# A residual block ended row tile by row tile: how the output projection hands over to the feed-forward

## The chip, the cores and the metric

The kernel runs on one core of a Trainium2 chip. The metric is the device time of one execution in microseconds (us). The kernel before was run three times: 2187.65 us median, 2186.25 lowest, 2188.59 highest. One more execution was profiled; it took 2188.95 us, of which the profile's span covers 2187.3.

## The reference, cut to what matters

The reference chains two transformer blocks over 256 tokens of width 2048, all in fp32. The change sits in the second block, between its output projection and its feed-forward:

```python
x  = x + gt1 * (y @ w_out)                       # residual, 256 x 2048
h2 = rmsnorm_2(x, g_norm2) * (1 + sc2) + sh2     # needs all 2048 columns of a row
u  = h2 @ w_up                                   # 2048 x 11008
x  = x + gt2 * ((silu(conv3x3(u_gate) + conv_b) * u_val) @ w_down)
return rmsnorm_2(x, g_final)
```

`rmsnorm_2` divides each row by the root of the mean of its squares, so a row's norm waits for the last column block of the projection, but no row waits for another row.

## The kernel before, in words

**Tiles.** The 256 tokens are two row tiles `rt` of 128. A product of 256 x 2048 with a column block of 512 is cut into 8 units. A unit is 256 rows of the weight, two slices `kk` of 128. Every fp32 operand is split in two fp32r parts, high and low, and a product takes three matmuls of 128 x 512 (high-high, high-low, low-high). So a unit is 2 slices x 2 row tiles x 3 = 12 matmuls, a block is 96, and they add up in one PSUM buffer `gemm_ps[:, bank, rt]`; blocks alternate between two buffers.

**Weights.** SyncE fetches each unit into one of 4 slots (`w_raw`). ScalarE writes the high part (`w_hi`, L624), VectorE the low part (`w_lo`, L1053). ScalarE may write a slot only when TensorE has finished the unit that had it before: unit n waits for `used` of unit n-4.

**Activations.** Rows are scaled by their inverse root (ScalarE, L641, `rows_set`), transposed by TensorE in groups of two 128-column chunks (L1890, `ps[:, g % 2]`, `tr_ps`), scaled and shifted by VectorE into `tmpT` (L1085, `tr_val`), copied to the high part `a_hi` by ScalarE (L635, `tr_hi`) and taken off to the low part `a_lo` by VectorE (L1093, `tr_lo`). Unit i of the feed-forward's first block needs group i.

**Order.** Each engine runs one list of instructions written out by hand; semaphores tie the lists together, and an engine waits at the first instruction whose semaphore isn't there. The output projection (`U_OUT2`) has 4 column blocks. After the fourth, VectorE multiplies each row tile by the gate and adds it to the residual (`last_block`, L1109 and L1110), ScalarE takes the squares of the last block (`last_square`, L775), VectorE sums the parts and finds the inverse root of both tiles (`sum_of_parts` and `roots`, L1104 and L1063 to L1070), ScalarE scales the rows, and TensorE transposes groups 0 and 1. Then the first feed-forward block begins, with group i+2 transposed after unit i. 21 more blocks and the down projection follow, back to back. The last block of the down projection is already taken tile by tile (`by_tile`, `tile_ps`): the last four units run for tile 0 and then for tile 1, and `tile_root` (L1114 on) finds each tile's root by itself.

Of the kernel before, what the change touches and what calls it, by code (L numbers as in the profile page):

```python
# [5 lines left out]
F32 = mybir.dt.float32  # L6
# [7 lines left out]
P = 128  # L14
# [199 lines left out]

class Count:
# [16 lines left out]
def build(nc, a):  # L232
# [102 lines left out]
    cw = at("cw", [P, 10 * FCH], F32, 200.75)  # L335
    cwr = at("cwr", [P, 4, P], F32, 202.5)
# [53 lines left out]
    with nc.Block() as block:  # L390
# [218 lines left out]
        def _(act):  # L609
# [352 lines left out]
            for c in range(DC):  # L962
                for i in range(2, 10):
                    if c == 0 and i - 2 >= Y_AHEAD:
                        turned("y", i - 2)
                    splits(U_OUT2 // SLOTS + 2 * c, i, i + 1)
# [5 lines left out]
            for rt in range(RT):  # L972
                last_square(rt, xres, lambda rt: y[:, rt, (DC - 1) * NBLK:DC * NBLK], 1)
# [22 lines left out]
            def ffn_block(b, par, start=2, finish=2):  # L996
                for i in range(2, 10):
                    if isinstance(b, int) and b == 0:
                        if i == 2:
                            act.wait_ge(S("root_set"), 3)  # L1000
                            scaled_rows(y, xres, 0)
                            scaled_rows(y, xres, 1)
                        if i in (4, 6):
                            scaled_rows(y, xres, i // 2)
                        turned("x2", i - 2)
# [7 lines left out]
            ffn_block(0, 0, 0, 0)  # L1013
# [24 lines left out]
            for rt in range(RT):  # L1038
                last_square(rt, x2_sb, lambda rt: squares[:, rt], 2)
                act.wait_ge(S("root_out"), rt + 1)  # L1040
# [5 lines left out]
        def _(dve):  # L1046
# [611 lines left out]
            for c in range(DC):  # L1658
                for i in range(2, 10):
# [5 lines left out]
                    splits(U_OUT2 // SLOTS + 2 * c, i, i + 1)  # L1665
# [751 lines left out]
```

## Time and profile before

| | us |
|---|---|
| median of three runs | 2187.65 |
| profiled execution | 2188.95 |
| its span | 2187.3 |
| TensorE busy (matmul) | 2138.5 |
| VectorE busy | 1493.5 |
| ScalarE busy | 1054.3 |
| last matmul of the output projection starts | 1434.45 |
| first feed-forward matmul starts | 1446.40 |
| first matmul of the second feed-forward block starts | 1473.72 |

Busy times are sums over the span. The last three rows are times from the span's start; between them lies the stretch that the change touches. The profile gives TensorE's granted clock as a fraction of its upper level of 2.4 GHz, so 0.50 is the lower level of 1.2 GHz.

### The profile page before, as it was taken

The page shows a single profiled execution, that of the slowest core. Times are in us where ns is not written, and L with a number is a line of the kernel's source. Part 1 is how long each engine was busy: PE and PEld are TensorE (multiplying, and loading weights), DVE is VectorE, ACT ScalarE, POOL GpSimd, SP SyncE. Part 2 cuts the span into 40 slices and gives each one's busy share as a digit, 9 for nine tenths or more (in the row PEclk, how much of TensorE's full clock was granted, in tenths as well). Part 3 has the DMA queues.
Part 4 walks back from the last instruction along what each step waited for, and adds up shares of the span by engine and source line. Part 5 has one row for each costly group of instructions (what it writes and reads, how often), then busy time and mean ns, then how long its engine had stood idle before and what let it go on. Part 6 is the DMA issues. An engine that isn't in the chain of part 4 may idle for free.

```text
span 2187.3 us, 28818 instructions
## 1 busy us (share of the span) xinstructions
PE 2138.5 (98%) x10067; PEld 1734.2 (79%) x10067; DVE 1493.5 (68%) x2213; ACT 1054.3 (48%) x1317; POOL 50.3 (2%) x97
## 2 busy tenths in 40 slices
PE   7999999999999999999999999989999999999998
PEld 6777778888787777877788887868888888888886
DVE  6456657967676787776665777567787777775454
ACT  5343435654444444445633655445555555554443
POOL 0000000000001100000000000000000000000000
PEclk9999999999999999999999999989999999999999
DMA  8877768967777969976443436555556565567664
GB/s 313 280 274 252 261 237 286 345 237 261 240 275 250 334 222 353 320 257 203 144 125 103 134 108 221 185 194 185 181 183 191 177 198 177 183 194 244 192 194 141
DMA packets 279801, 484.18 MB, mean 221 GB/s; under 512 B 21630, under 2 KB 112864, under 8 KB 277648
## 3 DMA queue, kind: packets, MB, share of 16 engines
q1 hardware_dynamic: 274544, 464.93, 63.7%
q0 software_dynamic: 5152, 17.84, 2.3%
q8 instruction: 67, 1.10, 0.2%
q14 instruction: 38, 0.31, 0.0%
HBM read 476.23 MB, written 6.48 MB: 221 GB/s over the span
## 4 chain that ended last, share of the span: by engine, by line
PE 86%; DVE 6%; issue 3%; DMA 3%; ACT 2%; SPq 0%; ACTq 0%; DVEq 0%
PE gemm_ps L1805 75%; DVE w_lo L1053 2%; DMA w_raw<-in_w_in_dram 2%; ACT w_hi L624 2%; PE ps L1849 1%; DMA w_raw<-in_w_out_dram 1%; PE ps L2213 1%; DVE tmpT L1085 1%; PE ps L2351 1%; DVE msum L1220 1%; PE ps L2282 1%; PE ps L1890 0%; PE ps L2236 0%; PE ps L2235 0%; PE ps L1858 0%
## 5 line engine op out<-in xcount | busy, mean ns | idle before, releaser
L1053 DVE TENSOR_TENSOR w_lo<-w_raw,w_hi 128x1024 fp32r<-128x1024 f32 (+1 forms) x688 | 827.4, 1215 | 467.8 <-ACT w_hi L624 461.2
L1805 PE MATMUL gemm_ps<-w_hi,a_hi 128*128 128x512 f32 (+1 forms) x2304 | 916.4, 398 | 18.2 <-DVE w_lo L1053 9.3
L624 ACT ACTIVATE w_hi<-w_raw 128x1024 fp32r<-128x1024 f32 (+1 forms) x688 | 710.1, 1050 | 464.5 <-PE gemm_ps L1805 325.5
L1805 PE MATMUL gemm_ps<-w_hi,a_lo 128*128 128x512 f32 (+1 forms) x2304 | 897.1, 389 | 0.0
L1805 PE MATMUL gemm_ps<-w_lo,a_hi 128*128 128x512 f32 (+1 forms) x2304 | 896.1, 389 | 0.0
L1805 PEld LDWEIGHTS gemm_ps<-w_hi,a_hi 128*128 128x128 f32 x2304 | 434.3, 188 | 133.8 <-issue 25.5
L1805 PEld LDWEIGHTS gemm_ps<-w_hi,a_lo 128*128 128x128 f32 x2304 | 433.8, 188 | 91.9
L1805 PEld LDWEIGHTS gemm_ps<-w_lo,a_hi 128*128 128x128 f32 x2304 | 434.7, 189 | 84.2 <-issue 0.5
L1708 DVE SCALAR_TENSOR_TENSOR acc<-gp,cw,acc 128x256 f32<-128x256 f32 x344 | 151.5, 481 | 13.8 <-DVE acc L1708 1.4
L1220 DVE SCALAR_TENSOR_TENSOR msum<-mraw,cs,msum 128x1024 f32<-128x1024 f32 x120 | 153.3, 1277 | 1.2 <-DMA mraw<-in_w_mod_dram 0.4
L1805 PE MATMUL gemm_ps<-w_hi,ft_hi 128*128 128x512 f32 x344 | 134.2, 390 | 2.2 <-DVE w_lo L1053 2.2
L1805 PE MATMUL gemm_ps<-w_lo,ft_hi 128*128 128x512 f32 x344 | 133.9, 389 | 0.0
L1805 PE MATMUL gemm_ps<-w_hi,ft_lo 128*128 128x512 f32 x344 | 133.8, 389 | 0.0
L1805 PEld LDWEIGHTS gemm_ps<-w_hi,ft_hi 128*128 128x128 f32 x344 | 64.6, 188 | 16.3 <-issue 1.5
L1805 PEld LDWEIGHTS gemm_ps<-w_hi,ft_lo 128*128 128x128 f32 x344 | 64.6, 188 | 13.6
L1805 PEld LDWEIGHTS gemm_ps<-w_lo,ft_hi 128*128 128x128 f32 x344 | 64.6, 188 | 13.2
L1011 ACT ACTIVATE ub<-gemm_ps 128x1024 f32<-128x1024 f32 x22 | 22.6, 1029 | 91.3 <-PE gemm_ps L1805 91.3
L635 ACT ACTIVATE a_hi<-tmpT 128x512 fp32r<-128x512 f32 x40 | 25.3, 631 | 78.8 <-DVE tmpT L1085 78.8
L1085 DVE TENSOR_SCALAR tmpT<-ps,vec 128x256 f32<-128x256 f32 x80 | 37.8, 515 | 23.3 <-PE ps L1890 23.2
L722 ACT ACTIVATE br<-gemm_ps,stat 128x512 f32<-128x512 f32 x24 | 15.2, 684 | 50.8 <-PE gemm_ps L1805 50.8
L988 ACT ACTIVATE gp<-ps 128x256 f32<-128x256 f32 x43 | 14.3, 384 | 49.9 <-PE ps L2351 49.9
L1805 PE MATMUL gemm_ps<-w_hi,ys_hi 128*128 128x512 f32 x96 | 37.6, 392 | 0.0
(392 smaller groups left out, 1433.9 us busy)
## 6 DMA issues: line engine op xcount, KB each, us to landing
w_raw<-in_w_in_dram SPq DMA_DIRECT2D x336, 512.0 KB, 4.6
mraw<-in_w_mod_dram SPq DMA_DIRECT2D x192, 512.0 KB, 6.1
w_raw<-in_w_up_dram SPq DMA_DIRECT2D x336, 256.0 KB, 3.1
w_raw<-in_w_down_dram SPq DMA_DIRECT2D x84, 512.0 KB, 4.3
w_raw<-in_w_out_dram SPq DMA_DIRECT2D x64, 512.0 KB, 5.1
w_raw<-in_w_up_dram SPq DMA_DIRECT2D x24, 512.0 KB, 5.5
x_d<-xres POOLq DMA_DIRECT2D x2, 2048.0 KB, 8.4
x_sb<-in_x_dram SPq DMA_DIRECT2D x2, 1024.0 KB, 6.0
```

What stands on the lines that cost most here:

```text
L624: act.activation(w_hi[:, slot, :, 0:n], raw[:, slot, :, 0:n], ACT.Copy).then_inc(hi_done, 1)
L635: act.activation(a_hi[:, UK * g:UK * g + UK], tmp[:, g % 2], ACT.Copy).then_inc(S("tr_hi"), 1)
L1011: act.activation(ub[:, par], gemm_ps[:, par], ACT.Copy).then_inc(evac_act, 1)
L1053: dve.tensor_tensor(w_lo[:, slot, :, 0:n], raw[:, slot, :, 0:n], w_hi[:, slot, :, 0:n].bitcast(F32), ALU.subtract).then_inc(lo_done, 1)
L1085: ins = dve.tensor_scalar(tmpT[:, g % 2, k], bank[:, k * T:(k + 1) * T], scale[:, kc:kc + 1], b, ALU.mult, ALU.add if bias is not None els ...
L1220: dve.scalar_tensor_tensor(out=msum[:], in0=row, scalar=cs[:, j, 0:1], in1=msum[:], op0=ALU.mult, op1=ALU.add).then_inc(sum_used, 1)
L1708: ins = dve.scalar_tensor_tensor(out=a_f, in0=gp[:, f, dy:dy + 4, dx:dx + 64], scalar=cw[:, bass.ds(tap * FCH + (b - 1) * 2 + f, 1)], in1=a_f,
L1805: mm = pe.matmul(gemm_ps[:, bank, rt, 0:n], x[:, chunk0 + k, rt * P:(rt + 1) * P], w[:, slot, kk, 0:n], start=(k == 0 and part == 0), stop ...
L1849: mm = pe.matmul(pD[32 * g:32 * g + 32, :], cs[:, k], mraw[:, i, kk], start=(k < 4), stop=(k >= KC - 4), skip_group_check=True)
L2213: pe.matmul(numb[d][:, rt * GDV:(rt + 1) * GDV], mpT[:, at0:at0 + P], v[t][:, h * GDV:(h + 1) * GDV], start=(n == 0), stop=(n == len(seen) ...
L2282: mm = pe.matmul(pC[:, l % 4 * P:(l % 4 + 1) * P], key, query, start=True, stop=True)
L2351: mm = pe.transpose(bank[:, f * T + rt * P:f * T + (rt + 1) * P], ub[:, 1 - par, rt, c0:c0 + P], ident)
```

## The change

1. The fourth block of the output projection ends by tile: its last four units run for tile 0 (then `tile_ps`), then for tile 1. VectorE ends tile 0's residual and its root while tile 1 is multiplied.
2. The 8 transposition groups become 12. Groups 0 to 3 are chunks 0 to 7 of tile 0, groups 4 to 7 the same of tile 1, groups 8 to 11 chunks 8 to 15 of both tiles. Group 0's transposes stand in the middle of the projection's last unit, group 1's right behind it. Groups 1 and 3 are scaled and shifted by ScalarE itself (`own=True`).
3. The feed-forward's first block runs units 0 to 3 for tile 0 (6 matmuls each), then units 0 to 3 for tile 1, then units 4 to 7 for both. `used` of units 0 to 3 comes only with tile 1.
4. ScalarE's and VectorE's lists for this stretch are written out anew, the splits of feed-forward units 0 to 9 among them.
5. `tile_root`, which also ends the kernel, has a shorter chain: one instruction for the first guess in place of two, two factors set without waiting, two refinement steps in place of three, the second of higher order.

```diff
+def seam_turn(g):
+    if g < BU:
+        return (g // 4,), g % 4
+    return (0, 1), g - 4
+SEAM_ROWS = ((0, 0), (0, 1), (1, 0), (1, 1), (0, 2), (1, 2), (0, 3), (1, 3))
 @@ ScalarE, after the output projection
+            def seam_rounded(g, own=False):
+                tiles, pair = seam_turn(g)
+                G = BU * tr_use["x2"] + g
+                cols = slice(tiles[0] * P, (tiles[-1] + 1) * P)
+                n = len(tiles) * P
+                if own:
+                    act.wait_ge(S("tr_ps"), G + 1)
+                    if g >= 2:
+                        act.wait_ge(S("tr_lo"), G - 1)
+                    for k in range(UK):
+                        kc = UK * pair + k
+                        ins = act.activation(tmpT[:, g % 2, k, 0:n], ps[:, g % 2, k * n:(k + 1) * n], ACT.Identity,
+                                             scale=vec[:, 140 + kc:141 + kc], bias=vec[:, 124 + kc:125 + kc])
+                    ins.then_inc(S("tr_val"), 1)
+                act.wait_ge(S("tr_val"), G + 1)
+                act.activation(a_hi[:, UK * pair:UK * pair + UK, cols], tmpT[:, g % 2, :, 0:n], ACT.Copy).then_inc(S("tr_hi"), 1)
+            last_square(0, xres, square_junk, 1)
+            seam_split(0)
+            seam_rows((0, 0))
+            seam_split(1)
+            seam_rounded(0)
+            seam_rounded(1, own=True)
+            seam_rows((0, 1))
+            last_square(1, xres, square_junk, 1)
+            seam_split(2)
+            seam_rounded(2)
+            seam_rounded(3, own=True)
+            seam_split(3)
+            seam_rows((1, 0))
+            seam_rounded(4)
+            seam_rows((1, 1))
+            seam_rounded(5)
+            seam_rounded(6)
+            seam_rows((0, 2), (1, 2))
+            seam_split(4)
+            seam_rounded(7)
+            seam_rounded(8)
+            seam_rows((0, 3), (1, 3))
+            seam_split(5)
+            seam_rounded(9)
+            for i in range(6, 10):
+                if i < 8:
+                    seam_rounded(4 + i)
+                seam_split(i)
 @@ VectorE, tile_root
-                me(dve.tensor_scalar(r.bitcast(I32), t.bitcast(I32), 1, None, ALU.logical_shift_right))
-                me(dve.tensor_scalar(r.bitcast(I32), r.bitcast(I32), -1.0, float(ROOT_BITS), ALU.mult, ALU.add))
-                me(dve.tensor_scalar(h, t, -0.5, None, ALU.mult))
-                for _ in range(3):
-                    me(dve.scalar_tensor_tensor(out=u, in0=r, scalar=h, in1=r, op0=ALU.mult, op1=ALU.mult))
-                    me(dve.scalar_tensor_tensor(out=r, in0=u, scalar=1.5, in1=r, op0=ALU.add, op1=ALU.mult))
+                dve.tensor_scalar(h, t, -0.5, None, ALU.mult)
+                dve.tensor_scalar(k, t, 0.375 ** 0.5, None, ALU.mult)
+                me(dve.tensor_scalar(r.bitcast(I32), t.bitcast(I32), -0.5, float(ROOT_BITS), ALU.mult, ALU.add))
+                me(dve.scalar_tensor_tensor(out=u, in0=r, scalar=h, in1=r, op0=ALU.mult, op1=ALU.mult))
+                me(dve.scalar_tensor_tensor(out=r, in0=u, scalar=1.5, in1=r, op0=ALU.add, op1=ALU.mult))
+                me(dve.scalar_tensor_tensor(out=u, in0=r, scalar=k, in1=r, op0=ALU.mult, op1=ALU.mult))
+                me(dve.scalar_tensor_tensor(out=u, in0=u, scalar=-1.25 / 0.375 ** 0.5, in1=u, op0=ALU.add, op1=ALU.mult))
+                me(dve.scalar_tensor_tensor(out=r, in0=u, scalar=1.875, in1=r, op0=ALU.add, op1=ALU.mult))
+                dve.engine_nop().then_inc(S("root_out"), 1)
 @@ VectorE, after the output projection
+            last = slice((DC - 1) * NBLK, D)
+            dve.wait_ge(S("tile_ps"), 1)
+            last_block(0, xres, (DC - 1) % 2, gtb, gated2)
+            tile_root(0, 1)
+            seam_split(0)
+            seam_turned(0)
+            dve.wait_ge(used, U_FFN)
+            multiplied = me.begin(dve.tensor_tensor(gated2[:, 1], gemm_ps[:, (DC - 1) % 2, 1], gtb[:, last], ALU.mult))
+            seam_rest(0)
+            dve.wait_ge(S("dve_own"), multiplied)
+            dve.tensor_tensor(xres[:, 1, last], xres[:, 1, last], gated2[:, 1], ALU.add).then_inc(evac_dve, 1)
+            seam_rest(1)
+            seam_split(1)
+            seam_turned(2)
+            seam_split(2)
+            seam_rest(2)
+            tile_root(1, 1)
+            seam_rest(3)
+            seam_split(3)
+            seam_turned(4)
+            seam_turned(5)
+            seam_rest(4)
+            seam_rest(5)
+            seam_turned(6)
+            seam_rest(6)
+            seam_turned(7)
+            seam_split(4)
+            seam_rest(7)
+            seam_turned(8)
+            seam_split(5)
+            seam_rest(8)
+            seam_turned(9)
+            seam_rest(9)
+            for i in range(6, 10):
+                if i < 8:
+                    seam_turned(4 + i)
+                    seam_rest(4 + i)
+                seam_split(i)
 @@ TensorE, product()
+                if tile_first:
+                    for rt in range(RT):
+                        for i in range(tile_first):
+                            parts_in(i, (rt,))
+                            pe.wait_ge(lo_done, u0 + i + 1)
+                            for kk in range(UK):
+                                mm = part_of_unit(i, kk, rt)
+                            if rt:
+                                mm.then_inc(used, 1)
+                            after(i, (rt,))
+                        if late and (i, kk) == (units - 1, 0):
+                            late()
 @@ TensorE, after the output projection
+                        by_tile=SLOTS if c == DC - 1 else 0, late=(lambda: seam_turns(0)) if c == DC - 1 else None)
+            seam_turns(1)
+            def seam_parts(i, tiles):
+                g = 4 * tiles[0] + i if i < 4 else 4 + i
+                pe.wait_ge(S("tr_lo"), BU * tr_use["x2"] + g + 1)
+            def seam_after(i, tiles):
+                seam_turns(*{(0, 0): (2,), (1, 0): (3,), (3, 0): (4, 5), (0, 1): (6,), (1, 1): (7,), (2, 1): (8,), (3, 1): (9,)}.get(
+                    (i, tiles[0]) if i < 4 else None, (6 + i,) if i in (4, 5) else ()))
+            pe.wait_ge(evac_dve, 19)
+            product(U_FFN, 0, 0, a_hi, a_lo, BU, after=seam_after, parts_in=seam_parts, tile_first=4)
```

Here `seam_turned(g)` is VectorE's scale and shift of group g, `seam_rounded(g)` ScalarE's copy to the high part, `seam_rest(g)` VectorE's low part, `seam_split(i)` the high (ScalarE) or low (VectorE) part of weight unit i, `seam_rows((rt, c))` the scaling of column block c of tile rt, and `seam_turns(g)` TensorE's transposes. A one-tile group has 2 transposes, 128-wide scalings and 128x256 high and low parts; a two-tile group has 4 transposes and sizes twice as wide.

## Rows read from the trace of the kernel before

**Rows 1.** The page: busy time by engine, its share of the span, instructions

```profile
PE 2138.5 (98%) x10067; PEld 1734.2 (79%) x10067; DVE 1493.5 (68%) x2213; ACT 1054.3 (48%) x1317; POOL 50.3 (2%) x97
```

**Rows 2.** Windows: stretch, busy us of PE, PEld, DVE, ACT, POOL, clock, DMA

```profile
1435.00:1440.00 5.00, 0.00 (x0) 0.00 (x0) 3.84 (x12) 1.45 (x4) 0.75 (x1) 0.75 0.18 77
...
1445.00:1450.00 5.00, 3.60 (x9) 2.83 (x10) 3.33 (x5) 4.28 (x6) 0.56 (x1) 0.50 0.61 224
```

**Rows 3.** Timeline of TensorE in that stretch; start, us, engine, line, instruction, wait before

```profile
1417.68 0.39 PE L1805 MATMUL gemm_ps<-w_hi,a_hi 128*128 128x512 f32 x1
...
1434.45 0.39 PE L1805 MATMUL gemm_ps<-w_hi,a_lo 128*128 128x512 f32 x1
1442.83 1.94 PE L1890 MATMUL ps<-cst,xn 128*128 128x128 f32 x8 [8.00 <-ACT xn L641]
1446.40 0.79 PE L1805 MATMUL gemm_ps<-w_hi,a_hi 128*128 128x512 f32 x1 [1.62 <-DVE a_lo L1093]
...
1451.44 0.60 PE L1890 MATMUL ps<-cst,xn 128*128 128x128 f32 x4
1451.80 0.47 PE L1805 MATMUL gemm_ps<-w_hi,a_hi 128*128 128x512 f32 x1
...
1470.87 0.50 PE L1805 MATMUL gemm_ps<-w_hi,a_hi 128*128 128x512 f32 x1
...
1473.72 0.39 PE L1805 MATMUL gemm_ps<-w_hi,a_hi 128*128 128x512 f32 x1
```

**Rows 4.** Timeline of VectorE in that stretch

```profile
1434.88 0.69 DVE L1109 TENSOR_TENSOR sg<-gemm_ps,gtb 128x512 f32<-128x512 f32 x1 [3.06 <-PE gemm_ps L1805]
...
1447.17 1.22 DVE L1053 TENSOR_TENSOR w_lo<-w_raw,w_hi 128x1024 fp32r<-128x1024 f32 x1
1448.30 0.68 DVE L1093 TENSOR_TENSOR a_lo<-tmpT,a_hi 128x512 fp32r<-128x512 f32 x1
1452.08 1.00 DVE L1085 TENSOR_SCALAR tmpT<-ps,vec 128x256 f32<-128x256 f32 x2 [3.10 <-PE ps L1890]
```

**Rows 5.** Timeline of ScalarE in that stretch

```profile
1441.36 2.56 ACT L641 ACTIVATE xn<-xres,stat 128x512 f32<-128x512 f32 x4 [2.92 <-DVEq L1099]
...
1456.30 0.63 ACT L635 ACTIVATE a_hi<-tmpT 128x512 fp32r<-128x512 f32 x1 [1.61 <-DVE tmpT L1085]
1456.84 1.05 ACT L624 ACTIVATE w_hi<-w_raw 128x1024 fp32r<-128x1024 f32 x1
```

**Rows 6.** Timeline of VectorE at the kernel's end, where tiles are already taken singly

```profile
2172.29 0.69 DVE L1109 TENSOR_TENSOR tmp_dn<-gemm_ps,gt2b 128x512 f32<-128x512 f32 x1 [2.45 <-PE gemm_ps L1805]
...
2175.44 0.22 DVE L1123 SCALAR_TENSOR_TENSOR stat<-stat 128x1 f32<-128x1 f32 x1
2175.70 0.16 DVE L1124 SCALAR_TENSOR_TENSOR stat<-stat 128x1 f32<-128x1 f32 x1
```

**Rows 7.** Timeline of ScalarE at the kernel's end

```profile
2173.74 0.63 ACT L775 ACTIVATE squares<-x_sb 128x512 f32<-128x512 f32 x1 [5.16 <-DVE x_sb L1110]
...
2176.90 1.15 ACT L1041 ACTIVATE x_sb<-x_sb,stat 128x1024 f32<-128x1024 f32 x1 [2.43 <-DVEq L1777]
```

**Rows 8.** Instructions grouped by shape, whole span; busy us, mean ns

```profile
L1504 DVE TENSOR_SCALAR mpT<-ps,sx 128x256 f32<-128x256 f32 x24 | 10.1, 478 | 23.6 <-PE ps L2182 14.3 <-PE ps L2217 9.3
L1504 DVE TENSOR_SCALAR mpT<-ps,sx 128x128 f32<-128x128 f32 x8 | 2.7, 343 | 0.0
L1193 DVE TENSOR_TENSOR ys_lo<-yT,ys_hi 128x256 fp32r<-128x256 f32 x12 | 5.0, 418 | 0.0
L992 ACT ACTIVATE acc<-gp,cw 128x256 f32<-128x256 f32 x43 | 23.6, 595 | 3.4 <-ACT gp L988 3.3
```

**Rows 9.** Clock elsewhere: small matmuls on TensorE, then windows of 1 us

```profile
996.71 2.73 PE L2121 MATMUL ps<-sx,cst 128*128 128x4 f32 x24
...
703.00:704.00 1.00, 0.09 (x1) 0.00 (x0) 0.98 (x1) 0.57 (x1) 0.00 (x0) 1.00 0.63 182
...
1001.00:1002.00 1.00, 1.00 (x4) 0.81 (x3) 1.00 (x2) 0.00 (x0) 0.00 (x0) 0.50 1.09 430
```

More of the change, by code:

```diff
@@ L224, in __call__, with begin @@
         self.eng.wait_ge(self.sem, self.n + self.off)
+    def begin(self, ins):
+        self.n += 1
+        ins.then_inc(self.sem, 1)
+        return self.n
     def iteration(self, first, i):
@@ L965, in _ @@
                         turned("y", i - 2)
-                    splits(U_OUT2 // SLOTS + 2 * c, i, i + 1)
+                    if c < DC - 1 or i < BU:
+                        splits(U_OUT2 // SLOTS + 2 * c, i, i + 1)
                     if c == 0:
@@ L971, in _, with seam_rows @@
                         squares_of(c - 1, xres, lambda rt: y[:, rt, (c - 1) * NBLK:c * NBLK])
-            for rt in range(RT):
-                last_square(rt, xres, lambda rt: y[:, rt, (DC - 1) * NBLK:DC * NBLK], 1)
+            def seam_rows(*places):
+                for rt, c in places:
+                    cols = slice(c * NBLK, (c + 1) * NBLK)
+                    act.wait_ge(S("root_out"), rt + 1)
+                    act.activation(y[:, rt, cols], xres[:, rt, cols], ACT.Identity,
+                                   scale=stat[:, 34 + rt:35 + rt]).then_inc(S("rows_set"), 1)
@@ L1687, in _, with seam_turned @@
                 dve.tensor_tensor(xres[:, :, cols], xres[:, :, cols], sg[:], ALU.add).then_inc(evac_dve, 1)
-            sum_of_parts(1)
-            roots()
+            def seam_turned(g):
+                tiles, pair = seam_turn(g)
+                G = BU * tr_use["x2"] + g
+                n = len(tiles) * P
+                dve.wait_ge(S("tr_ps"), G + 1)
+                if g >= 2:
+                    dve.wait_ge(S("tr_hi"), G - 1)
+                for k in range(UK):
+                    kc = UK * pair + k
+                    ins = dve.tensor_scalar(tmpT[:, g % 2, k, 0:n], ps[:, g % 2, k * n:(k + 1) * n], vec[:, 140 + kc:141 + kc],
+                                            vec[:, 124 + kc:125 + kc], ALU.mult, ALU.add)
+                ins.then_inc(S("tr_val"), 1)
@@ new lines, in seam_rest, with seam_split @@
+            def seam_rest(g):
+                tiles, pair = seam_turn(g)
+                cols = slice(tiles[0] * P, (tiles[-1] + 1) * P)
+                dve.wait_ge(S("tr_hi"), BU * tr_use["x2"] + g + 1)
+                own = slice(UK * pair, UK * pair + UK)
+                dve.tensor_tensor(a_lo[:, own, cols], tmpT[:, g % 2, :, 0:len(tiles) * P], a_hi[:, own, cols].bitcast(F32),
+                                  ALU.subtract).then_inc(S("tr_lo"), 1)
+            def seam_split(i):
+                split(U_FFN // SLOTS + i // SLOTS, i % SLOTS)
@@ L1781, in _ @@
             tile_root(1, 2)
-            dve.engine_nop().then_inc(S("root_out"), 1)
             scaled_right(1)
@@ L1808, in part_of_unit @@
                     return mm
-                for i in range(units):
+                if tile_first:
[8 more added lines that the diff above has]
+                            after(i, (rt,))
+                for i in range(tile_first, units):
+                    if parts_in:
+                        parts_in(i, (0, 1))
                     if turned:
@@ L2329, in second_vectors, with seam_turns @@
                     mm.then_inc(S("cw_ps"), 1)
+            def seam_turns(*groups):
+                for g in groups:
+                    tiles, pair = seam_turn(g)
+                    G = BU * tr_use["x2"] + g
+                    n = len(tiles) * P
+                    pe.wait_ge(S("tr_val"), G - 1)
+                    pe.wait_ge(S("rows_set"), DC * len(ROWS) + seam_rows_before(g))
+                    for k in range(UK):
+                        from_col = (UK * pair + k) * P
+                        for at_tile, rt in enumerate(tiles):
+                            mm = pe.transpose(ps[:, g % 2, k * n + at_tile * P:k * n + (at_tile + 1) * P], y[:, rt, from_col:from_col + P], ident)
+                    mm.then_inc(S("tr_ps"), 1)
             for c in range(DC):
@@ L2359, in ffn_block @@
                 product(U_FFN + BU * b, 0, par, a_hi, a_lo, BU, n=n,
-                        turning=("x2", y, 0) if isinstance(b, int) and b == 0 else None,
                         after=lambda u: turn_u(b, par, turned) if u == 3 and turned else None)
-            ffn_block(0, 0, 0)
             ffn_block(1, 1)
```

57 lines of the change are left out of this document (25 added, 32 removed).

## The prediction

> **What bounds the kernel now.** I read the page first: TensorE is busy for 2138.5 of 2187.3 us [rows 1]. So almost nothing is to be had outside the few stretches in which TensorE stands still, and a delay anywhere else is hidden unless it makes TensorE wait. Then the windows: from 1435 to 1440 TensorE does nothing at all and the clock falls from 1.00 to 0.50 within the stretch (mean 0.75); from 1445 to 1450 it works at 0.50, which is 1.2 GHz [rows 2]. Then the timelines. The last matmul of the output projection starts at 1434.45, the first of the feed-forward at 1446.40, and in between are only 8 transposes [rows 3]. At the full clock matmuls follow each other every 0.2266 us (1417.68 to 1434.45 is 74 of them), so a unit of 12 takes 2.72; the feed-forward's first unit took 5.04 (1446.40 to 1451.44), 2.3 lost to the low clock. Later units come every 3.2, bound by TensorE: 2.72 and some 0.45 for four transposes. The second block begins at 1473.72. With no wait at all it could begin about 1434.68 + 96 x 0.2266 + 8 x 0.45 = 1460.0. That is the prize: 13.7 us at most, 0.6%. Behind 1473.72 nothing but work follows, so a shift there passes on to the end.
>
> **Durations.** All from rows of before, waits between engines (0.02 to 0.05, 0.13 from rows to transposes) as they stand there.
> - Weight unit: high part 1.05, and 0.95 if something follows at once; low part 1.22, then 1.13 [rows 4, 5].
> - Scaling rows: four in 2.56, so 0.64 each, 0.71 alone [rows 5].
> - Two-tile group: four transposes 0.36 plus 0.09 on the next matmul, 0.64 from their start to VectorE [rows 3, 4]; scale and shift 1.00 (then 0.91); high part 0.63, then 0.54; low part 0.69, then 0.60 [rows 4, 5].
> - One-tile group: two transposes 0.18, so 0.46 to VectorE. Its scale and shift is not in the trace. Halving a read of 256 saves 135 ns (478 to 343) [rows 8]; off the 0.50 each of the wide pair that is 0.37, 0.73 the pair, 0.64 if followed. Bounds: 0.50 the pair (half the wide one) and 1.00 (no saving). Low part 0.42 [rows 8], 0.33 followed; high part 0.42, as the weight's 1.05 for 1024 less the 0.63 for 512 gives 0.42 for 512 and hence 0.21 less for 256.
> - ScalarE's own scale and shift with a per-partition scale and bias: 0.595 at 256 wide [rows 8], less 0.107 for 128 columns is 0.49, the pair 0.89. Bounds 0.60 and 1.19.
> - Root of one tile: at the end it takes 4.61 from the multiply (2172.29) to ScalarE's scaling (2176.90) [rows 6, 7]. Removed are one step of 0.19 and a refinement of 0.26 + 0.20 [rows 6]; one step of 0.19 is added to the second refinement, `h` no longer waits and `k` comes beside it (about nothing together). Saved: 0.45, bounds 0.2 and 0.6.
>
> **The sum, part by part**, by program order on each engine.
>
> *To the first feed-forward matmul.* The units' order changes nothing for TensorE: the 24 matmuls of tile 1 hide tile 0's ending. Tile 0's last matmul starts at 1434.45 - 24 x 0.2266 = 1429.01. Multiply at 1429.47; 4.61 - 0.45 later ScalarE scales rows, 1433.63; 0.71 + 0.13, transposes at 1434.47. TensorE came to them at 1434.00: a wait of 0.5. Three matmuls remain, the last at 1435.27; VectorE multiplies tile 1 0.43 later [rows 3, 4], then group 0's low part at 1436.30 (0.60 on), and 0.42 + 0.05 later the feed-forward starts: **1436.77, 9.6 us earlier.**
>
> *Tile 0, units 0 to 3.* From here TensorE is fed by chains of VectorE and ScalarE. ScalarE's own group 1: transposes seen 1435.96, 0.89, then 0.44: VectorE's low part 1437.31, weight unit 1's at 1437.64, its matmuls at 1438.9. ScalarE goes on with rows, the square of tile 1, the high part of unit 2 (1438.58 to 1439.63). VectorE: low part of unit 2 at 1439.65, group 2's at 1440.78, then the root of tile 1 from 1441.11 (1.83) before group 3's low part (1442.94) and unit 3's (1443.27 + 1.22 + 0.05). Unit 3 starts at 1444.54; TensorE waited 0.5, 0.7 and 1.9.
>
> *Turn to tile 1.* Groups 4 and 5 are queued behind unit 3 on TensorE: 1444.54 + 1.36 = 1445.90. To VectorE 0.46, two scalings 1.28, low part 0.47: unit 0 of tile 1 at 1448.11, a wait of 1.8.
>
> *To unit 4.* Group 6's transposes at 1449.47. Then one chain to the end of the tile part: 0.46 to VectorE, 0.69 scaling, 0.33 high part, 1.31 two rows, 1.07 high part of unit 4, 1.13 its low part, 0.33 group 7's low part, 1.02 group 8's scaling, 0.54 its high part, 1.30 two rows, 1.07 high part of unit 5, 1.13 its low part, 0.73 group 8's low part. That is 11.1: unit 4 starts at 1460.58. On VectorE group 8's low part is queued behind weight unit 5's, which ScalarE makes only behind two rows that nobody needs yet. TensorE, done with unit 3 of tile 1 and group 9 at about 1456.6, waits 4.0 us.
>
> *To the second block.* Group 10 is transposed behind unit 4: 2.72 + 0.64. In the last two turns each list is scale, low part, weight: 1.02 + 0.54 + 1.07 + 1.13 for unit 6, then 1.02 + 0.54 + 1.07 + 1.27 for unit 7: 7.7, against TensorE's 3.2 a turn before. Unit 7 starts at 1471.6, where it started at 1470.87 [rows 3]. **So the 9.6 us are all given back: 0.7 us later.** The trailing splits (units 8, 9) end about 1473.9, just in time for 1474.5; SyncE's fetches follow the same low parts, each with at least a unit's time in hand.
>
> *The kernel's end.* Tile 1's root is on the path: -0.45. Net so far +0.3.
>
> *The clock.* Before, it fell once and cost 2.3, and that is in 1473.72. Now the 4.0 us wait before unit 4 is the longest. Before, TensorE stood still from 1434.85 and the window 1435 to 1440 averages 0.75, so it fell within about 2.7 us [rows 2, 3]. I take the fall as certain there. Unit 4's twelve matmuls are on the path, since group 10 waits behind them: 12 x 0.2 = +2.4 (bounds 1.0, if it rises within the unit, and 2.9). And earlier? From 1442.6 to 1448.1 TensorE works 1.7 of 5.5 us. A wait of 1.7 us around 703 to 705 left the clock at 1.00, but at 1001 it was 0.50 behind 24 matmuls of 4 columns (996.71 to 999.4) without any wait [rows 9]: it can fall without a standstill. I take a second fall as likely; it doubles unit 0 of tile 1 and part of unit 1, and the rest hides beside the 11.1 chain: +1.5 (bounds 0 and 3).
>
> The Trainium skill speaks against this change here: "TensorE: Matmul & The Clock Gate", section "A second HAM failure mode: psum-queue depth-cycling", says that short idles between groups of matmuls make the clock go back and forth between its levels. The trace agrees at 1001 and not at 703; by that rule the second fall is sure and the sum is the one below, without it 1.5 less.
>
> **Sum:** +0.3 + 2.4 + 1.5 = +4.2. On the profiled execution 2188.95 + 4.2 = 2193.15; it lies 1.3 above the median, so the median becomes **2191.9**. Its own bounds: the steps on the chain (some 50, each known to 0.03) give 1.5 either way, the clock +1.0 to +5.9 in place of 3.9.
>
> **Rivals.**
> 1. *One fall only*, at the long wait: +2.7, 2190.4. For it 703 to 705, against it 1001. Chance 0.25.
> 2. *No fall at all*: +0.3, 2188. Only if 4 us of standstill go by unseen; against it all of 1435 to 1440. Chance 0.05.
> 3. *The long wait isn't there* (faster). If ScalarE gets to the high part of weight unit 5 while VectorE is still at unit 4's, group 8's low part comes as TensorE is done with unit 3, at 1456.6 and not at 1460.6: -4.0, both falls go, and the last two turns stay at TensorE's 3.2 (-1.3): +0.3 - 5.3 = -5.0, 2182.7. It decides at the start of unit 4: before 1457. Against it stands the order of the lists; for it only that 50 steps laid by hand may hide a slack. Chance 0.16.
> 4. *The feed is slower than laid*: the narrow instructions at their upper bounds (0.27 on each of six VectorE pairs, 0.3 on each of ScalarE's two), four of them on the chain, and both falls at full price (+2): +7.5, 2195. Chance 0.10.
> 5. The forecast, two falls: 0.44.
>
> **Numbers.** 0.2% is 4.4 us, about what a measurement tells from none. The forecast lies just inside it, so 0.18 of its 0.44 is slower; of rival 4 nearly all (0.10), of rival 1 0.02: slower 0.30. Faster: rival 3 beyond -4.4, 0.16. Same: 0.54. Range 2184.5 to 2196: it leaves out most of rival 3 and the far end of 4.
>
> **What would show it.** The first feed-forward matmul within 0.5 of 1436.8; waits of TensorE of about 1.9, 1.8 and 4.0 before unit 3 of tile 0, unit 0 of tile 1 and unit 4; VectorE's low part of weight unit 5 right ahead of group 8's low part; unit 4 at half clock; the second block starting 3 to 6 us later than 1473.72. I am wrong if unit 4 starts before 1457, if the clock stays at 1.00 through the stretch, or if the end moves by more than the second block's start less 0.45.

## The result: 3.5 us slower, where 4.2 were forecast, and the profile after

The changed kernel takes 2190.81 us (median of 20 runs, 2189.60 to 2193.73), the kernel before 2187.34 (median of 20, 2185.20 to 2190.09) in the same comparison: a ratio of 1.0016, 95% interval 1.0010 to 1.0022. Three later comparisons of the same two kernels gave 1.0008, 1.0007 and 1.0007 (intervals from 0.9998 to 1.0017). Over all comparisons the changed kernel's 53 runs have a mean of 2190.3 and the 124 of before one of 2188.1. Taken comparison by comparison, the means differ by 3.5, 1.6, 2.1 and 1.5 us, together 2.4. So the change costs 2.2 to 2.4 us, and the first measurement had drawn a high value.

The profiled execution of the changed kernel took 2190.47 us, its span 2188.8. The page's row answers to [rows 1]. TensorE's busy time comes out the same only as a sum of opposites. From an instruction that both kernels have (VectorE's multiply at 1413.12 before, 1414.07 after) to the end of the feed-forward's first block (1473.92 and 1475.92) TensorE is busy for 51.1 of 60.8 us before and for 50.1 of 61.9 us after. It stands still 2.0 us longer and works 1.0 us less, in a profile in which its clock didn't fall there.

```profile
PE 2138.7 (98%) x10067; PEld 1732.4 (79%) x10067; DVE 1494.5 (68%) x2225; ACT 1056.3 (48%) x1325; POOL 50.5 (2%) x97
```

TensorE in the changed stretch, answering to [rows 3] (the last column is the idle time before the row and what ended it):

```profile
1435.30 0.41 PE L2491 MATMUL ps<-cst,xn 128*128 128x128 f32 x2 [0.20 <-ACT xn L1005]
1437.57 0.47 PE L1938 MATMUL gemm_ps<-w_hi,a_hi 128*128 128x512 f32 x1 [0.94 <-issue]
...
1445.39 0.47 PE L1938 MATMUL gemm_ps<-w_hi,a_hi 128*128 128x512 f32 x1 [1.69 <-DVE w_lo L1131]
...
1449.03 0.50 PE L1938 MATMUL gemm_ps<-w_hi,a_hi 128*128 128x512 f32 x1 [1.57 <-DVE a_lo L1789]
...
1455.97 0.50 PE L1938 MATMUL gemm_ps<-w_hi,a_hi 128*128 128x512 f32 x1 [1.22 <-DVE a_lo L1789]
...
1457.47 0.60 PE L2491 MATMUL ps<-cst,xn 128*128 128x128 f32 x4
1461.58 0.50 PE L1938 MATMUL gemm_ps<-w_hi,a_hi 128*128 128x512 f32 x1 [3.51 <-DVE a_lo L1789]
...
1464.44 0.60 PE L2491 MATMUL ps<-cst,xn 128*128 128x128 f32 x4
1469.09 0.47 PE L1938 MATMUL gemm_ps<-w_hi,a_hi 128*128 128x512 f32 x1 [0.84 <-DVE w_lo L1131]
...
1472.88 0.47 PE L1938 MATMUL gemm_ps<-w_hi,a_hi 128*128 128x512 f32 x1 [0.81 <-DVE w_lo L1131]
...
1475.72 0.39 PE L1938 MATMUL gemm_ps<-w_hi,a_hi 128*128 128x512 f32 x1
```

The one standstill of 8.00 and the 1.62 behind it are gone. In their place are ten shorter ones; those shown add up to 10.8, two of 0.41 and 0.37 are left out. All but one name VectorE or ScalarE as what ended them; the 0.94 names nothing (`issue`) and ends as group 0's low part does on VectorE (1437.46). TensorE is fed from hand to mouth until the second block.

VectorE and ScalarE around the longest wait, the 3.51 before unit 4 (L1789 is `seam_rest`, L1131 the low part of `seam_split`, L1779 `seam_turned`; L1005 scales rows, L650 makes a weight's high part, L1024 is `seam_rounded`), answering to [rows 4, 5]:

```profile
1455.83 0.99 DVE L1779 TENSOR_SCALAR tmpT<-ps,vec 128x256 f32<-128x256 f32 x2
1459.69 1.23 DVE L1131 TENSOR_TENSOR w_lo<-w_raw,w_hi 128x1024 fp32r<-128x1024 f32 x1 [2.87 <-ACT w_hi L650]
1460.84 0.68 DVE L1789 TENSOR_TENSOR a_lo<-tmpT,a_hi 128x512 fp32r<-128x512 f32 x1
```

```profile
1456.86 0.63 ACT L1024 ACTIVATE a_hi<-tmpT 128x512 fp32r<-128x512 f32 x1 [2.23 <-DVE tmpT L1779]
1457.40 1.32 ACT L1005 ACTIVATE xn<-xres,stat 128x512 f32<-128x512 f32 x2
1458.62 1.04 ACT L650 ACTIVATE w_hi<-w_raw 128x1024 fp32r<-128x1024 f32 x1
```

Read the two fences together. Group 8's high part is there at about 1457.5, and its low part (0.68, the last thing unit 4 needs) starts only at 1460.84. Between them VectorE is idle for 2.87 us: its list has the low part of weight unit 5 first, and that waits for ScalarE, which scales two rows (1457.40) before it makes the high part (1458.62). Unit 4 needs neither the rows nor weight unit 5.

The chain at the end, answering to [rows 6, 7], VectorE's last multiply and ScalarE's last scaling:

```profile
2179.00 0.69 DVE L1187 TENSOR_TENSOR tmp_dn<-gemm_ps,gt2b 128x512 f32<-128x512 f32 x1 [0.74 <-PE gemm_ps L1938]
```

```profile
2183.28 1.15 ACT L1119 ACTIVATE x_sb<-x_sb,stat 128x1024 f32<-128x1024 f32 x1 [2.10 <-DVEq L1205]
```

They are 4.28 apart. For the second tile before, it was 4.78 (2176.98 to 2181.76).

### The profile page after: what moved, and what is told of

Same layout as the page of the kernel before. It is cut to its first block, busy times and chain, and to the rows that moved or that the text cites. A ratio compares the mean times of both kernels' runs of the same rounds, so it can differ in the third digit from the quotient of the medians.

```text
span 2188.8 us, 28849 instructions
## 1 busy us (share of the span) xinstructions
PE 2138.7 (98%) x10067; PEld 1732.4 (79%) x10067; DVE 1494.5 (68%) x2225; ACT 1056.3 (48%) x1325; POOL 50.5 (2%) x97
## 4 chain that ended last, share of the span: by engine, by line
PE 85%; DVE 6%; issue 3%; DMA 3%; ACT 3%; SPq 0%; ACTq 0%; DVEq 0%
PE gemm_ps L1938 75%; DVE w_lo L1131 2%; ACT w_hi L650 2%; DMA w_raw<-in_w_in_dram 2%; PE ps L1998 1%; DMA w_raw<-in_w_out_dram 1%; PE ps L2362 1%; DVE tmpT L1163 1%; PE ps L2530 1%; DVE msum L1301 1%; PE ps L2431 1%; PE ps L2385 0%; PE ps L2384 0%; PE ps L2007 0%; PE ps L2296 0%
## 5 line engine op out<-in xcount | busy, mean ns | idle before, releaser
L1131 DVE TENSOR_TENSOR w_lo<-w_raw,w_hi 128x1024 fp32r<-128x1024 f32 (+1 forms) x688 | 827.2, 1215 | 468.2 <-ACT w_hi L650 461.7
L650 ACT ACTIVATE w_hi<-w_raw 128x1024 fp32r<-128x1024 f32 (+1 forms) x688 | 710.1, 1050 | 457.3 <-PE gemm_ps L1938 321.5
L661 ACT ACTIVATE a_hi<-tmpT 128x512 fp32r<-128x512 f32 x32 | 20.2, 631 | 69.1 <-DVE tmpT L1163 69.1
L1163 DVE TENSOR_SCALAR tmpT<-ps,vec 128x256 f32<-128x256 f32 x64 | 29.8, 508 | 15.8 <-PE ps L2039 15.7
L1075 ACT ACTIVATE gp<-ps 128x256 f32<-128x256 f32 x43 | 14.3, 384 | 50.1 <-PE ps L2530 50.1
```

The costliest lines, as they stand in the source:

```text
L650: act.activation(w_hi[:, slot, :, 0:n], raw[:, slot, :, 0:n], ACT.Copy).then_inc(hi_done, 1)
L661: act.activation(a_hi[:, UK * g:UK * g + UK], tmp[:, g % 2], ACT.Copy).then_inc(S("tr_hi"), 1)
L1131: dve.tensor_tensor(w_lo[:, slot, :, 0:n], raw[:, slot, :, 0:n], w_hi[:, slot, :, 0:n].bitcast(F32), ALU.subtract).then_inc(lo_done, 1)
L1163: ins = dve.tensor_scalar(tmpT[:, g % 2, k], bank[:, k * T:(k + 1) * T], scale[:, kc:kc + 1], b, ALU.mult, ALU.add if bias is not None els ...
```

## The experiments

**How they are compared.** In medians of 11 runs of these kernels 1 us is noise, and the profiled executions differ by up to 4.6 us before the changed stretch even begins (tile 0's multiply starts between 1425.75 and 1430.39). So I measure a stretch *S* inside each profile: from VectorE's multiply of tile 0 to ScalarE's first eviction of the first feed-forward block (`ub`). The kernel before multiplies tile 0 only behind tile 1's 24 matmuls; its S is counted from 5.41 us earlier, the moment at which the changed order lets VectorE start (1434.88 - 5.41 = 1429.47, as laid out; measured from the multiply at 1413.12 and 1414.07 that both have, it is 5.44, which would make S of the kernel before 0.03 longer). These are the ends of S in the changed kernel, and below them its end in the kernel before:

```profile
1430.39 0.69 DVE L1187 TENSOR_TENSOR gated<-gemm_ps,gtb 128x512 f32<-128x512 f32 x1 [3.06 <-PE gemm_ps L1938]
```

```profile
1475.92 1.03 ACT L1060 ACTIVATE ub<-gemm_ps 128x1024 f32<-128x1024 f32 x1 [2.56 <-PE gemm_ps L1938]
```

```profile
1473.92 1.03 ACT L1011 ACTIVATE ub<-gemm_ps 128x1024 f32<-128x1024 f32 x1 [3.22 <-PE gemm_ps L1805]
```

So S is 45.53 after and 44.45 before. From `ub` to the end of the span every kernel with the new root takes 712.80 to 712.90 and every one with the old root 713.33 to 713.38. S, with 0.5 for the tail, therefore carries the whole difference; ahead of tile 0's multiply only the order of the projection's last units differs, and S allows for it. All results in one table ("low" is how many us inside S the granted clock was 0.50; "long wait" is the one before unit 4):

| kernel | S | low | long wait | median of runs, us | ratio to before, 95% |
|---|---|---|---|---|---|
| before, first profile | 44.45 | 13.7 | - | 2187.34 | 1 |
| e5 before again | 43.93 | 10.2 | - | 2189.46 | 1.0006, 0.9997 to 1.0015 |
| e6 before, new root | 44.21 | 10.2 | - | 2187.45 | 0.9993, 0.9984 to 1.0003 |
| e7 before, kept busy | 41.88 | 0 | - | 2185.97 | 0.9990, 0.9981 to 0.9999 |
| after, first profile | 45.53 | 0 | 3.51 | 2190.81 | 1.0016, 1.0010 to 1.0022 |
| e1 after again | 47.12 | 3.4 | 3.48 | 2189.41 | 1.0008, 0.9999 to 1.0017 |
| e9 after again | 48.23 | 6.8 | 3.52 | 2190.44 | 1.0007, 0.9998 to 1.0016 |
| e12 after again | 47.14 | 3.4 | 3.51 | 2189.70 | 1.0007, 0.9998 to 1.0016 |
| e2 long wait filled | 45.48 | 0 | 0.52 | 2188.80 | 1.0006, 0.9997 to 1.0015 |
| e3 all waits filled | 45.55 | 0 | 0.55 | 2188.31 | 1.0001, 0.9992 to 1.0010 |
| e4 unit 5 first | 42.57 | 0 | 0.55 | 2185.62 | 0.9990, 0.9981 to 0.9999 |
| e10 turns ahead | 46.11 | 6.8 | 3.54 | 2189.17 | 1.0003, 0.9994 to 1.0012 |
| e11 last turns | 45.48 | 3.4 | 3.50 | 2188.53 | 1.0004, 0.9995 to 1.0013 |
| e8 all lists | 37.52 | 0 | none | 2180.50 | 0.9965, 0.9951 to 0.9979 |

That e5, an unchanged kernel, reads 1.0006 is the measure of what a ratio says here.

**e1, e9, e12: the changed kernel again.** No edit. The first profile had shown the long wait with the clock at 1.00 throughout, against the forecast; was that the rule?

> The changed kernel once more, unchanged. Theory A (the clock): the handovers alone cost +0.6 us against the kernel before, and the other 2.9 of the measured +3.5 come from executions in which the clock falls in TensorE's 3.5 us wait before unit 4, as it did not in the execution that was profiled. So +3.5 in the median, and this profile, with luck, shows such a fall: unit 4 in 5.0 us and not 2.9. Theory B (elsewhere): the extra is spread over the kernel, from the moved fetches or from the start; +3.5 as well, but the second block begins at most 1.5 us later than in the kernel before, whatever the clock does.

> The changed kernel unchanged, a third profile of it. From tile 0's ending to the end of the feed-forward's first block it took 45.5 us without a fall of the clock and 47.1 with one in the long wait; it must be one of the two. If falls come only there, the shorter waits again show 1.00.

> The changed kernel once more, for a fourth profile and more timed runs: 45.5 or 47.1 us for the stretch, and a median 1 to 3 us above the kernel before.

It was the exception. Windows of the first profile, of e1 and of e9 around unit 4 (the last three columns are the granted clock, the DMA share and GB/s):

```profile
1457.00:1462.00 5.00, 1.49 (x9) 1.07 (x8) 2.31 (x4) 2.66 (x4) 0.00 (x0) 1.00 0.30 102
```

```profile
1456.00:1461.00 5.00, 4.06 (x11) 3.24 (x12) 2.48 (x5) 0.63 (x1) 0.00 (x0) 0.66 0.35 105
```

```profile
1460.00:1467.00 7.00, 6.51 (x19) 5.16 (x19) 2.30 (x5) 0.63 (x1) 0.00 (x0) 0.54 0.24 75
```

and TensorE's unit 4 in e9, from its first matmul to the transposes behind its twelfth:

```profile
1460.49 0.80 PE L1938 MATMUL gemm_ps<-w_hi,a_hi 128*128 128x512 f32 x1 [3.52 <-DVE a_lo L1789]
...
1465.78 0.91 PE L2491 MATMUL ps<-cst,xn 128*128 128x128 f32 x4
```

That is 5.29 us for a unit that took 2.86 in the first profile (1461.58 to 1464.44). Every wait in the three repeats agrees with the first profile within 0.05; only the clock differs. The fall comes with the 3.5 us wait in e1, e9, e12, e10 and e11 and is missing in the first profile: 5 of 6, or 3 of 4 for this kernel alone. It costs 1.6 twice (47.12 and 47.14 against 45.53) and 2.7 once (48.23). In e12 the clock came down only about 1.0 us after the wait had ended: unit 4's first matmuls, from 1459.70, still have the full clock.

```profile
1459.70 0.50 PE L1938 MATMUL gemm_ps<-w_hi,a_hi 128*128 128x512 f32 x1 [3.51 <-DVE a_lo L1789]
...
1460.75 0.63 PE L1938 MATMUL gemm_ps<-w_lo,a_hi 128*128 128x512 f32 x1
```

Of the expectations, e1's +3.5 in the median was too high (2189.41 against 2188.18 beside it), e9's 48.23 is neither of the two values named, and e12 came out as expected.

**e2 and e3: fill the waits.** TensorE multiplies into an unused PSUM bank while it would stand still; outputs are untouched.

```diff
+            def keep_busy(n, slot):
+                for _ in range(n):
+                    pe.matmul(ps[:, 3], a_hi[:, 0, 0:P], w_hi[:, slot, 0], start=True, stop=True)
 @@ seam_after, behind the transposes (e2; e3 has also 7, 6 and 4 of them at (2, (0,)), (3, (0,)), (2, (1,)))
+                if (i, tiles) == (3, (1,)):
+                    pe.wait_ge(lo_done, U_FFN + 5)
+                    keep_busy(13, 0)
```

> The changed kernel with 13 extra matmuls of 128x512 on TensorE in the long wait (behind group 9's transposes, 13 x 0.2266 = 2.9 of the 3.5 us idle), into a PSUM bank that nobody reads. They add work and no result. Theory A: the clock can't fall there, so -2.0 to -2.9 us against the changed kernel, about +0.6 to +1.5 against the one before. Theory B: no change, +3.5.

> As the one before, and in the three shorter waits too: 7 matmuls before unit 3 of tile 0, 6 before unit 0 of tile 1, 4 before unit 3 of tile 1. If a second fall in the earlier waits is part of the cost, as forecast (+1.5), this gains up to 1.5 us more than the long wait's filling alone; if falls come only in the long wait, it is the same as that within 0.3.

TensorE in e2, the filling and unit 4:

```profile
1456.18 3.24 PE L2515 MATMUL ps<-w_hi,a_hi 128*128 128x512 f32 x13
1459.94 0.50 PE L1938 MATMUL gemm_ps<-w_hi,a_hi 128*128 128x512 f32 x1 [0.52 <-DVE a_lo L1789]
```

With the long wait filled unit 4 begins at the full clock and S is 45.48, as in the profile without a fall. So the fall and nothing else makes 47.12 and 48.23 of it. Filling the shorter waits too adds nothing (45.55): they never brought the clock down, neither here nor in any of the seven profiles that have them unfilled (waits of 0.2 to 1.7 us). The runs moved less than the -2.0 to -2.9 us expected of e2: medians of -0.6 (e2) and -1.1 us (e3) against e1, in the same direction and too close to settle it. Against the runs of before beside them their means are +1.1 and +0.6, where S less the tail says +0.8. What settles it is the profiles, one of each.

**e7: the same filling in the kernel before.** 34 matmuls before the first two groups' transposes and 8 behind them.

```diff
+                    if turning[0] == "x2":
+                        keep_busy(34)
                     for g in range(ahead, 2):
                         turn(*turning, g)
+                    if turning[0] == "x2":
+                        keep_busy(8)
```

> The kernel before with 34 extra matmuls of 128x512 in the 8 us wait at the end of the projection and 8 in the wait behind the first transposes. They add work and no result. It prices the clock in the kernel before: the first unit in 2.72 in place of 5.04, transposes at full clock, so -2.3 to -2.9 us against the kernel before if the fall comes in every execution; 0 if the low clock there was hidden by the feed.

```profile
1445.63 0.50 PE L1814 MATMUL gemm_ps<-w_hi,a_hi 128*128 128x512 f32 x1 [0.20 <-DVE a_lo L1093]
...
1448.48 0.60 PE L1899 MATMUL ps<-cst,xn 128*128 128x128 f32 x4
```

The first unit takes 2.85 where it took 5.04 [rows 3], S falls by 2.3 (against the mean 44.20 of the three profiles of before) and the mean time by 2.2. This gives the comparison that the first result hid. Without any fall on either side the change costs 45.53 - 41.88 = 3.65 in the stretch. Before pays about 2.3 for its fall in each of its three profiles, the changed kernel 1.5 on average: part of the loss was covered by one fall exchanged for another.

**e5, e6: before again, and before with the new root alone.** e6 is the kernel before with the changed `tile_root` body, which there acts only at the kernel's end.

```diff
-                for _ in range(3):
+                me(dve.scalar_tensor_tensor(out=u, in0=r, scalar=k, in1=r, op0=ALU.mult, op1=ALU.mult))
+                me(dve.scalar_tensor_tensor(out=u, in0=u, scalar=-1.25 / 0.375 ** 0.5, in1=u, op0=ALU.add, op1=ALU.mult))
+                me(dve.scalar_tensor_tensor(out=r, in0=u, scalar=1.875, in1=r, op0=ALU.add, op1=ALU.mult))
```

> The kernel before, unchanged, for a second profile of it. Its median must come out at the kernel before's (within 1 us); what is asked is the profile: theory A says that the clock falls in its 8 us wait in every execution and costs 2 to 3 us each time, so from the projection's end to the end of the feed-forward's first block it takes 44.2 to 45 us as in the profile of before (44.5, counted from where tile 0's last matmul ends).

> The kernel before with nothing but the shorter root of one tile, which it uses at its end alone. Forecast and the profile of the changed kernel: -0.5 us, seen as 4.28 in place of 4.78 us from the last multiply to ScalarE's last scaling; in the timed median -0.5, too small to be told from none. Rival, that the order of the list makes the tail wait elsewhere: 0.

```profile
2177.67 0.69 DVE L1109 TENSOR_TENSOR tmp_dn<-gemm_ps,gt2b 128x512 f32<-128x512 f32 x1 [0.73 <-PE gemm_ps L1807]
```

```profile
2181.95 1.15 ACT L1041 ACTIVATE x_sb<-x_sb,stat 128x1024 f32<-128x1024 f32 x1 [2.10 <-DVEq L1784]
```

4.28 apart, as after: the tail's -0.50 is the root's alone. e5 just missed both of its marks, with a median 1.05 above that of before, where 1 was allowed, and an S of 43.93, where 44.2 to 45 was expected: so wide is the scatter of a kernel that nobody changed. The median of e6 lies 1.0 below that of before, which the interval doesn't tell from nothing.

**e4: undo the queueing before unit 4.** One line moves in ScalarE's list.

```diff
             seam_rounded(7)
+            seam_split(5)
             seam_rounded(8)
             seam_rows((0, 3), (1, 3))
-            seam_split(5)
```

> The changed kernel with one move in ScalarE's list: the high part of weight unit 5 ahead of group 8's high part and of two scalings of rows, which nobody needs yet. VectorE's list stays. Queue theory: unit 4 starts at once behind group 8's low part, about 1458.6 in place of 1461.6, so -2.9 us, and what the clock costs in the long wait goes with it: -3 to -5.5 against the changed kernel, so between +0.5 and -2.2 against the one before. Rival: TensorE only waits later, for unit 6, since VectorE is the bound there: under 1 us.

```profile
1455.61 0.60 PE L2491 MATMUL ps<-cst,xn 128*128 128x128 f32 x4
1456.76 0.50 PE L1938 MATMUL gemm_ps<-w_hi,a_hi 128*128 128x512 f32 x1 [0.55 <-DVE a_lo L1789]
```

The wait of 3.5 becomes 0.55, the clock stays up, and S is 42.57: 2.96 less than the changed kernel without a fall. The median is 2185.62: 2.6 below before and 3.8 below e1, both on the same chip. Against before, the medians give a little more than was expected at best (-2.2), the means just that (-2.2). One instruction of 1.04 us in the wrong place was more than the whole loss against before. The rival, that TensorE would only wait later, didn't come: before units 6 and 7 it waits 0.87 and 0.81, as it did (0.84 and 0.81).

**e10: transpose groups 4 and 5 one unit earlier. e11: the last two turns make the weight first.** In e10 TensorE does them behind unit 2 of tile 0 and not behind unit 3. VectorE's added wait makes sure that group 3's low part is written before group 5 takes its buffer. In e11 both lists end with weight unit 6 ahead of group 10 and unit 7 ahead of group 11; the fence shows VectorE's, ScalarE's is changed in the same way.

```diff
-                seam_turns(*{(0, 0): (2,), (1, 0): (3,), (3, 0): (4, 5), ...
+                seam_turns(*{(0, 0): (2,), (1, 0): (3,), (2, 0): (4, 5), ...
 @@ VectorE
             seam_turned(4)
+            dve.wait_ge(S("tr_lo"), BU * tr_use["x2"] + 4)
             seam_turned(5)
```

```diff
-            for i in range(6, 10):
-                if i < 8:
-                    seam_turned(4 + i)
-                    seam_rest(4 + i)
-                seam_split(i)
+            seam_split(6)
+            seam_turned(10)
+            seam_rest(10)
+            seam_split(7)
+            seam_turned(11)
+            seam_rest(11)
+            seam_split(8)
+            seam_split(9)
```

> The changed kernel with the transposes of groups 4 and 5 ahead of unit 3 of tile 0 on TensorE, where it waits 1.7 us for a weight anyway, and not behind it. Queue theory: the wait of 1.6 before tile 1 goes and all that follows comes 1.6 to 2.1 earlier. Rival: the wait moves to unit 1 of tile 1, under 0.5.

> The changed kernel with units 6 and 7's weight parts ahead of groups 10 and 11 in both lists. Queue theory: units 6 and 7 start 1.1 and 1.5 us earlier, so -1.5 against the changed kernel. Rival: VectorE is the bound there, 0.

TensorE in e10, at the turn to tile 1, and in e11, before unit 7:

```profile
1442.69 0.63 PE L2492 MATMUL ps<-cst,xn 128*128 128x128 f32 x4 [0.96 <-ACT xn L1005]
1443.42 0.47 PE L1939 MATMUL gemm_ps<-w_hi,a_hi 128*128 128x512 f32 x1
1444.95 0.50 PE L1939 MATMUL gemm_ps<-w_hi,a_hi 128*128 128x512 f32 x1
```

```profile
1465.81 0.48 PE L1943 MATMUL gemm_ps<-w_hi,a_hi 128*128 128x512 f32 x1
...
1469.11 0.51 PE L1943 MATMUL gemm_ps<-w_hi,a_hi 128*128 128x512 f32 x1 [0.30 <-DVE a_lo L1791]
```

In e10 the waits of 1.69 and 1.57 shrink to one of 0.96 ahead of the transposes; unit 3 of tile 0 (1443.42) and unit 0 of tile 1 (1444.95) begin without one. Both kernels keep the long wait and its fall, so each is held against a repeat with as long a fall: e10 saves 48.23 - 46.11 = 2.1, e11 47.13 - 45.48 = 1.65.

**e8: all of it.** e4's move, e10's, e11's in a stronger form, and two changes more: on ScalarE the rows for groups 5 and 8 are scaled one place earlier, on VectorE group 8's low part ahead of weight unit 5's. The stronger form: ScalarE makes the high part of weight unit 6 ahead of group 9's and that of unit 7 ahead of group 10's, and VectorE scales group 10 ahead of weight unit 6's low part. The diff shows what the single runs don't have, except ScalarE's moves of weight units 6 and 7, which it leaves out.

```diff
 @@ ScalarE
-            seam_rows((1, 0))
+            seam_rows((1, 0), (1, 1))
             seam_rounded(4)
-            seam_rows((1, 1))
             seam_rounded(5)
-            seam_rounded(6)
             seam_rows((0, 2), (1, 2))
+            seam_rounded(6)
             seam_split(4)
 @@ VectorE
             seam_turned(8)
-            seam_split(5)
             seam_rest(8)
+            seam_split(5)
             seam_turned(9)
             seam_rest(9)
+            seam_turned(10)
+            seam_split(6)
+            seam_rest(10)
```

> The changed kernel with the three lists put in another order and nothing added: groups 4 and 5 transposed ahead of unit 3 of tile 0 and not behind it; ScalarE's high parts of units 5, 6 and 7 and group 7 moved ahead of work that isn't needed yet; VectorE's group 8 low part ahead of unit 5's, group 10's scaling ahead of unit 6's low part. Queue theory, laid by hand: waits of 1.6 before tile 1, 1.2 before its unit 3, 3.5 before unit 4, and 0.8 twice in the last turns go but for 1.5 in all, the first block ends 8.8 us earlier, so -8 to -9 against the changed kernel and -7 to -8 against the one before. Rival: VectorE is the bound and the waits come back elsewhere: -3 to -5 against the changed kernel, as with unit 5 alone.

All of TensorE's waits from the turn to tile 1 on (0.97 and 0.33), and unit 7, which begins without one:

```profile
1442.34 0.63 PE L2496 MATMUL ps<-cst,xn 128*128 128x128 f32 x4 [0.97 <-ACT xn L1005]
...
1452.80 0.50 PE L1943 MATMUL gemm_ps<-w_hi,a_hi 128*128 128x512 f32 x1 [0.33 <-DVE a_lo L1790]
...
1462.51 0.50 PE L1943 MATMUL gemm_ps<-w_hi,a_hi 128*128 128x512 f32 x1
```

S is 37.52, 8.0 less than after and 6.7 less than before. The time is 2180.50 us (5 runs, 2178.63 to 2182.48) against 2188.41, faster by 7.7 in the means (ratio 0.9965), as was expected (-7 to -8): better than both kernels. Of the 8.0 the parts run singly give 2.96 + 2.12 + 1.65 = 6.7. The remaining 1.3 must come from what was not run by itself, that is the two changes and the stronger form, or from the parts acting together; which of these isn't shown. The waits show where it lies: the 1.22 before unit 3 of tile 1, which no single run touched, is 0.33 here, and the 0.55 that e4 left before unit 4 is gone.

## Why the prediction was right, and where it was not

The direction, the place and the mechanism of the queues were right; one of the two clock terms was wrong, the other too large, and the sum too large by about 2 us. That +4.2 came so near to the first measurement's +3.5 is in part luck, since all runs together give +2.2 to +2.4. Of the signs named in advance, one spoke against the forecast in the first profile: the clock stayed at 1.00 through the stretch, and the second block began 2.0 us later than before and not 3 to 6. Only the repeats showed the fall. Times of the first profile are given less 0.92, by which it lay late already at tile 0's multiply (1430.39 against 1429.47 laid out).

- *The schedule.* First feed-forward matmul 1436.65 (1436.77 laid out), unit 3 1444.47 (1444.54), unit 0 of tile 1 1448.11 (1448.11), unit 4 1460.66 (1460.58), unit 7 1471.96 (1471.6), second block 1474.80 (1474.5). A chain of some 50 steps, most of them read from rows of before, held to 0.1 until unit 4 and to 0.4 at its end; the last 0.3 came in the two last turns.
- *Narrow instructions.* VectorE's pair took 0.73 as estimated by halving the saving of a halved read; ScalarE's own pair 0.79 to 0.81 where 0.89 was taken.
- *The waits.* 0.41 and 0.37 before units 1 and 2 where 0.5 and 0.7 were laid out, then 1.69, 1.57 and 3.51 where it was 1.9, 1.8 and 4.0; a wait of 1.22 stands before unit 3 of tile 1, which the working went past since the chain that it followed didn't run through TensorE. So the long wait is 0.5 shorter and the start of unit 4 the same.
- *The tail.* -0.50, laid out -0.45.
- *The handovers* together: S 45.53 - 44.45 = +1.08, less 0.50, is +0.6 within the two first profiles, laid out +0.3; with the mean of before's three profiles (44.20) it is +0.8.
- *The fall in the long wait*: taken as certain at +2.4. It comes in 5 of 6 profiles and costs 1.6 or 2.7; over the changed kernel's four profiles 0, 1.6, 1.6 and 2.7, a mean of 1.5. The working had the price of a fall over the whole unit, and where the low clock lasted that long (e9) unit 4 took 5.29 - 2.86 = 2.4 more, as laid out. In e1 the clock rose again with about four matmuls of the unit left, as the lower bound allowed.
- *The second fall* in the earlier waits, "likely" at +1.5: wrong. It came in none of the seven profiles that have waits up to 1.7 us. I had given the one case in which the clock fell without a standstill (24 matmuls of 4 columns at 996.71 [rows 9]) more weight than the wait of 1.7 us at 703 that left it at 1.00 [rows 9]. The waits laid out here were like the second, and nothing in the stretch was like the first. The Trainium skill ("TensorE: Matmul & The Clock Gate", section "A second HAM failure mode: psum-queue depth-cycling") tells of another kernel that short idles between groups of matmuls made its clock go back and forth, and it gives no length for them. The working took this as a rule that makes the second fall sure, and took 1001 as agreeing with it, though the rows there show no idle, so that the case wasn't one of short idles. Here idles of 0.2 to 1.7 us lowered nothing, and the measurement decides.

The sum of what the profiles showed is +0.8 + 1.5 = +2.3, which agrees with the +2.2 to +2.4 of the timed runs. The likeliest case should have been the rival *one fall only* (+2.7, 2190.4; the pooled mean is 2190.3). Rival 3, the long wait that isn't there, is what e4 makes of the kernel. Apart from the falls it was priced at -5.3, e4 shows -2.96: the wait itself was 3.5 and not 4.0, 0.55 of it stays, and the last two turns stay slow (waits of 0.87 and 0.81) even with unit 4 early, where I had given them TensorE's own pace (-1.3). They needed e11's edit.

## What to carry to other kernels

On engines that run one list in order, splitting a handover into pieces gives only a head start. To keep it, each list must be in the order in which the fed engine needs the pieces, across all lists: here a head start of 9.6 us was lost, and 8.0 of it came back once instructions of about 1 us, whose results were needed only a unit or two later, stood behind what was needed at once. To find them, take each wait of the fed engine, see when the last input's own inputs were there, and read what its engine did in between. And price a clock fall only where the engine stands still for as long as it did at a fall that the trace shows, or works as it did at one; count it as a chance, not as a constant.

## What the runs showed of the hardware that was not expected

- The same wait of 3.5 us brought the granted clock down in three executions of one program and not in a fourth (with e10 and e11, in five of six), for 3.4 or for 6.8 us. In e12 it came down only when the wait was already over. Two profiles of an unchanged kernel can differ by 2.7 us in 47 for this alone, so a single profile of it can hide a term or invent one.
- Waits of up to 1.7 us, several in a row with a few matmuls between them, left it at 1.00 in every profile. The longer ones, 8.00 in the kernel before, brought it down in all three of its profiles. Behind the 24 matmuls of 4 columns [rows 9] it fell in 7 of the 14 profiles, for 3.4 us each time, without a standstill.
- VectorE steps that don't wait for each other start 0.07 apart, though each lasts 0.15:

```profile
1432.98 0.15 DVE L1197 TENSOR_SCALAR stat<-stat 128x1 f32<-128x1 f32 x1
1433.05 0.14 DVE L1198 TENSOR_SCALAR stat<-stat 128x1 f32<-128x1 f32 x1
```

  A step that waits for the one before starts 0.19 behind it (1432.79 to 1432.98). The new root's two factors together delay the next step by 0.13 (to 1433.11), less than one such step. The Trainium skill ("VectorE: DVE Perf Modes", section "The DRAIN you can't avoid") says that the next operation starts earlier where it isn't held, and the trace agrees in these two rows: 0.07 is less than the 0.15 of the first.
